# Windowed attention: the mask added in PSUM by VectorE, and the reciprocal denominators turned once and spread by DMAs

## The chip, the core and the metric

The kernel runs on one core of one Trainium2 chip. Its time is the device time of one execution in microseconds. A core has TensorE (matmuls and transposes, writing to PSUM), VectorE, ScalarE and GpSimd for elementwise work, and SyncE, which here only issues DMAs. The engines run their instructions in order and meet through semaphores.

## What is computed

Two layers of a diffusion trunk with 1,024 tokens of 1,024 features and 256 context tokens. Layer 0 mixes tokens by windowed attention with 16 query heads on 4 key/value heads, layer 1 by a Fourier mixer; each is followed by a mixture of 64 experts. The change is in layer 0's attention alone:

```
s = einsum('bqhgd,bkhd->bhgqk', qb, kk) * HEAD_DIM ** -0.5
s = where(abs(query - key) <= 128, s, -inf)          # window keys; context keys are unmasked
p = softmax(concatenate([s_window, s_context, sink], axis=-1))   # one sink logit per head, no value
out = p[window] @ v + p[context] @ v_ctx
y = out.reshape(B, L, 1024) @ w_o
```

## The kernel before

`attend` goes through 8 tiles of 128 queries and in each through 8 pairs of heads: 64 pairs. A pair has 384 window keys (256 in the first and last tile) and 256 context keys for each of its two heads. Pairs are even or odd, and each of the two kinds has its own PSUM buffer (`pair0`, `pair1`). A pair goes through these steps:

- TensorE: `scores(p)`, the products with the keys (L909 to L919) and then two bf16 matmuls with an identity, which add the mask of the outer key tiles (L923).
- VectorE: `largest(p, 0)` and `largest(p, 1)` (L795), the row maxima of the two heads, and `shift` (L804).
- ScalarE: `exps(p)`, two exponentials (L862) that write `prob` and its row sums.
- TensorE: `turn(p)`, ten transposes of 128x128 (eight in the edge tiles) into the same PSUM buffer (L934).
- VectorE and ScalarE: `copy(p)`, the first 512 columns and the rest to `pT` (L812, L870).
- TensorE: `values` (L954), once for two pairs: the part behind even pairs has twelve instructions in the trace, the part behind odd ones eight (four in the edge tiles).

The order is written out by hand. TensorE does `turn(p)`, at every fourth pair `denominators`, then `values`, then `scores(p + 2)`, which needs both copies of pair p. VectorE does `largest(p+1, 0)`, `copy(p)`, `largest(p+1, 1)`, `shift(p+1)`, and then at p = 2 of 4 `sinks`, at p = 3 of 4 `denominators`, at p = 1 of 4 `divide`. ScalarE does `copy(p)`, then `exps(p+1)`.

Four pairs are a group (8 heads), and there are 16. Its outputs lie transposed in PSUM (`att_o`, features on partitions, queries along the row), so its 8 reciprocal denominators per query must be brought into that shape. VectorE makes them (L827, 128x8), GpSimd spreads them to 128x512 (L782), TensorE transposes that in four pieces (`denominators`, L962), ScalarE copies it to `share` (`shares`, L879), and VectorE's `divide` multiplies (L833):

```
dve.wait_ge(share_done, n + 1)
dve.wait_ge(pv_mm, 4 * n + 4)
dve.tensor_tensor(oT[:, 4 * c:4 * c + 4, t * P:(t + 1) * P], psO[:], share[:], ALU.mult).then_inc(o_done, 1)
```

SyncE first loads `w_o` (L759), then fills scratch memory of the expert stages with zeros (L762 to L768), then loads the queries of tiles 2 to 7 (L754), each as soon as its buffer is free. When all engines have ended the attention, the next block begins with the output product (`mixY`, L1325).

Of the kernel before, what the change touches and what calls it, by code (L numbers as in the profile page):

```python
# [22 lines left out]
P = 128  # L23
D = 1024
# [179 lines left out]
def trunk(nc, A, out):  # L204
# [9 lines left out]
    with ExitStack() as whole:  # L214
# [481 lines left out]
        def attend(kT, v, w_o, oT, first_q, mask, sink):  # L696
# [6 lines left out]
            with ExitStack() as ctx:  # L703
                sb, ps, sem = pools(ctx)
                qT = first_q[:].rearrange("p (i k c) -> p i k c", i=2, k=KT)
                identb = sb("identb", [P, P], BF16)
# [4 lines left out]
                spread = sb("den_spread", [P, 4, 2, HD])  # L711
# [8 lines left out]
                far_mm, score_mm, max_done, exp_done = sem("far_mm"), sem("score_mm"), sem("max_done"), sem("exp_done")  # L720
                T_first, T_rest, copied_a, copied_d, pv_mm, o_done = (sem(n) for n in (
                    "probT_first", "probT_rest", "probT_a", "probT_d", "pv_mm", "o_done"))
                sink_in, sink_done, den_own, den_done, spread_done, den_mm, share_done = (sem(n) for n in (
                    "sink_in", "sink_done", "den_own", "den_done", "den_spread_done", "den_mm", "share_done"))
# [25 lines left out]
                with nc.Block(no_gpsimd_drain=True) as block:  # L750
                    @block.sync
                    def _(sp):
# [9 lines left out]
                        sp.dma_start(u_dram[DUMMY:, :].rearrange("p (h c) -> p h c", h=2),  # L762
                                     zero.unsqueeze(1).to_broadcast([P, 2, D // 2])).then_inc(zero_out, 16)
                        for l in range(DEPTH):
                            half = y_dram[l].rearrange("(n p j) (h c) -> j h p n c", p=P, j=2, h=2)
                            for h in range(2):
                                sp.dma_start(half[1, h], zero.unsqueeze(1).to_broadcast([P, YROWS // P, D // 2])).then_inc(zero_out, 16)
                                sp.dma_start(half[0, h, :, NT], zero).then_inc(zero_out, 16)  # L768
# [7 lines left out]
                    def _(pool):  # L776
                        pool.memset(zero, 0.0).then_inc(zeroed, 1)
                        pool.wait_ge(zeroed, 1)
                        for n in range(2 * NT):
                            pool.wait_ge(den_done, n + 1)  # L780
                            at_least(pool, den_mm, n)
                            pool.tensor_copy(spread[:], den[:].rearrange("p (a i) -> p i a", a=2).unsqueeze(3).to_broadcast([P, 4, 2, HD])  # L782
                                             ).then_inc(spread_done, 1)

                    @block.vector
                    def _(dve):
                        dve.tensor_copy(identb[:], ident[:]).then_inc(set_up, 1)
                        dve.tensor_scalar(nsink[:], sink[:], -1.0, None, ALU.mult).then_inc(set_up, 1)
                        dve.wait_ge(set_up, 2)

                        def largest(p, j):

                            dve.wait_ge(score_mm, p + 1)
# [26 lines left out]
                        def denominators(n):  # L820
# [3 lines left out]
                            at_least(dve, spread_done, n)  # L824
# [4 lines left out]
                        def divide(n):  # L829
                            t, c = n // 2, n % 2  # L830
                            dve.wait_ge(share_done, n + 1)
                            dve.wait_ge(pv_mm, 4 * n + 4)
                            dve.tensor_tensor(oT[:, 4 * c:4 * c + 4, t * P:(t + 1) * P], psO[:], share[:], ALU.mult).then_inc(o_done, 1)  # L833

                        largest(0, 0)
# [18 lines left out]
                    def _(act):  # L854
# [27 lines left out]
                        for p in range(N):  # L882
# [3 lines left out]
                            if p >= 4 and p % 4 == 0:  # L886
                                shares(p // 4 - 1)
# [1642 lines left out]
```

## Time and profile before

| | |
|---|---|
| Time, median of 3 runs | 2724.66 us (2721.68 to 2724.75) |
| Profiled execution | 2726.17 us, its span 2723.6 us |
| Granted TensorE clock, mean over the span | 0.985 |
| TensorE busy | 2614.6 us (96%) |
| VectorE, ScalarE, GpSimd busy | 2012.8, 1359.3, 613.1 us |
| The attention in the span | 253 to 520 us |

Starts are counted from the start of the span. Busy time of an engine is the time in which at least one of its instructions runs; matmuls overlap their neighbours, so the step from one start to the next is what one costs, and it is shorter than its duration. PE is TensorE, DVE VectorE, ACT ScalarE, POOL GpSimd, SPq the issuing of DMAs by SyncE. A clock of 1.00 is 2.4 GHz, 0.50 is 1.2 GHz.

### The profile page before, as it was taken

How to read it: one execution, taken by the hardware profiler on the slowest of the kernel's cores; microseconds unless marked ns; L12 is line 12 of the kernel's file. 1: busy time of each engine (PE TensorE's matmuls, PEld its weight loads, DVE VectorE, ACT ScalarE, POOL GpSimd, SP SyncE). 2: the span in 40 equal slices, each digit the busy share in tenths (PEclk: the TensorE clock that was granted, in tenths of full speed). 3: DMA queues.
4: the chain of work that ended last, by engine and by line, in shares of the span. 5: the costliest groups of instructions: out<-in, count | busy, mean ns of one | idle time of the engine just before them, and what ended most of it. 6: DMA issues, size and time to landing. Idle time of an engine off the chain costs nothing. (4 is left out here: it accounts for less than half of the span.)

```text
span 2723.6 us, 44405 instructions
## 1 busy us (share of the span) xinstructions
PE 2614.6 (96%) x14920; PEld 1176.8 (43%) x14923; DVE 2012.8 (74%) x5303; ACT 1359.3 (50%) x3150; POOL 613.1 (23%) x467
## 2 busy tenths in 40 slices
PE   7999999999899999999999889998999999999996
PEld 2444666544433333333444365444333343333342
DVE  4996666585588887788888465855898888888875
ACT  1112666343256666666666251431666666666651
POOL 0000000111023233233322221100233323233322
PEclk9999999999999999999999999999999999999998
DMA  9776500200399999999999732016999999999996
GB/s 366 266 266 200 187 17 17 76 39 39 146 371 368 332 337 353 327 337 377 352 334 339 248 146 84 39 47 241 362 366 340 343 318 341 335 372 332 338 345 205
DMA packets 151614, 697.65 MB, mean 256 GB/s; under 512 B 25505, under 2 KB 30881, under 8 KB 99162
## 3 DMA queue, kind: packets, MB, share of 16 engines
q1 hardware_dynamic: 103964, 555.09, 52.3%
q0 software_dynamic: 46832, 136.58, 20.3%
q10 hardware_dynamic: 592, 3.16, 0.3%
q8 instruction: 119, 1.95, 0.3%
q14 instruction: 107, 0.87, 0.1%
HBM read 597.50 MB, written 129.13 MB: 267 GB/s over the span
## 5 line engine op out<-in xcount | busy, mean ns | idle before, releaser
L1842 ACT ACTIVATE xT<-xt_blocks 32x256 f32<-32x256 f32 x2176 | 900.4, 414 | 39.0 <-DVE xt_blocks L1663 11.6
L1920 PE MATMUL exG<-ring,xT 128*32 128x512 f32 (+2 forms) x2608 | 572.1, 593 | 1.3 <-DMA ring<-in_exp_w_up_dram 0.7
L1678 DVE STREAM_TRANSPOSE ex_hT<-ex_h 32x64 f32<-32x64 f32 x2240 | 528.7, 236 | 33.6
L1920 PE MATMUL exG<-wide_w,xT 128*32 128x512 f32 (+2 forms) x1472 | 385.2, 600 | 0.7 <-DVE xT L1657 0.7
L1589 POOL DMA_INDIRECT y_scratch<-wide_w,idx_out x203 | 335.8, 1654 | 149.0 <-issue 66.6
L1920 PE MATMUL exG<-wide_t,xT 128*32 128x512 f32 (+2 forms) x960 | 361.5, 603 | 7.8 <-issue 4.4
L1576 POOL DMA_INDIRECT wide_t<-u_scratch,idx x144 | 152.6, 1060 | 937.8 <-DVE idx_out L1714 742.5
L1920 PEld LDWEIGHTS exG<-ring,xT 128*32 128x32 f32 (+2 forms) x2608 | 199.5, 129 | 314.7 <-issue 312.2
L1854 ACT ACTIVATE ex_e<-exG 128x256 f32<-128x256 f32 x142 | 54.4, 383 | 503.7 <-PE exG L1920 500.2
L1955 PE MATMUL exD<-ring,ex_hT 128*32 128x512 f32 (+2 forms) x1304 | 296.2, 597 | 2.5 <-DVE wide_w L1706 2.5
L1668 DVE TENSOR_TENSOR ex_h<-ex_e,exG 128x256 f32<-128x256 f32 x142 | 86.7, 611 | 190.9 <-ACT ex_e L1854 162.3
L1955 PE MATMUL exD<-wide_w,ex_hT 128*32 128x512 f32 (+2 forms) x736 | 197.4, 597 | 0.0
L1920 PEld LDWEIGHTS exG<-wide_w,xT 128*32 128x32 f32 (+2 forms) x1472 | 132.9, 134 | 146.9 <-issue 146.9
L1706 DVE SCALAR_TENSOR_TENSOR wide_w<-exD,w_all,mod 128x1024 f32<-128x1024 f32 x142 | 181.9, 1281 | 8.5 <-PE exD L1955 7.8
L1955 PE MATMUL exD<-wide_t,ex_hT 128*32 128x512 f32 (+2 forms) x480 | 181.9, 597 | 0.0
L1920 PEld LDWEIGHTS exG<-wide_t,xT 128*32 128x32 f32 (+2 forms) x960 | 111.0, 135 | 161.5 <-issue 158.8
L1628 DVE TENSOR_TENSOR mod<-place,slots 128x1024 bf16<-128x1024 f32 (+3 forms) x203 | 175.2, 888 | 3.5 <-PEq L235 2.5
L795 DVE TENSOR_REDUCE mx<-pair 128x1 f32<-128x640 f32 (+1 forms) x128 | 100.5, 786 | 95.0 <-PE pair L923 95.0
L1663 DVE STREAM_TRANSPOSE xt_blocks<-wide_t 128x1024 f32<-128x1024 f32 x136 | 168.1, 1236 | 2.3 <-DMA wide_t<-u_scratch,idx 2.3
L315 POOL TENSOR_TENSOR rstd<-var,halves 128x1 f32<-128x1 f32 x42 | 62.9, 1498 | 433.3 <-DVE var L301 433.3
L1955 PEld LDWEIGHTS exD<-ring,ex_hT 128*32 128x32 f32 (+2 forms) x1304 | 97.1, 129 | 115.7 <-issue 114.4
L1245 ACT ACTIVATE u2T<-mod 32x256 f32<-32x256 f32 x224 | 92.7, 414 | 108.1 <-DVE mod L1119 105.5
(369 smaller groups left out, 3275.8 us busy)
## 6 DMA issues: line engine op xcount, KB each, us to landing
ring<-in_exp_w_gate_dram SPq DMA_DIRECT2D x64, 1024.0 KB
ring<-in_exp_w_up_dram SPq DMA_DIRECT2D x64, 1024.0 KB
ring<-in_exp_w_down_dram SPq DMA_DIRECT2D x64, 1024.0 KB
wide_t<-in_exp_w_gate_dram SPq DMA_DIRECT2D x34, 1024.0 KB
wide_t<-in_exp_w_up_dram SPq DMA_DIRECT2D x34, 1024.0 KB
wide_t<-in_exp_w_down_dram SPq DMA_DIRECT2D x34, 1024.0 KB
wide_w<-in_exp_w_gate_dram SPq DMA_DIRECT2D x32, 1024.0 KB
wide_w<-in_exp_w_up_dram SPq DMA_DIRECT2D x32, 1024.0 KB
```

What stands on the lines that cost most here:

```text
L795: dve.tensor_reduce(mx[:, p % 2, j:j + 1], halves_of(p, pair[p % 2])[j], AX, ALU.max).then_inc(own, 1)
L1245: last = act.activation(uT[m * UNIT:(m + 1) * UNIT, t % DEEP, :, a * UNIT:(a + 1) * UNIT], parts[a * UNIT:(a + 1) * UNIT, m], ACT.Copy)
L1576: pool.indirect_dma_start(out=xg[:, par], out_offset=None, in_=u_dram, in_offset=bass.IndirectOffsetOnAxis(ap=idx[:, par:par + 1], axis=0) ...
L1589: pool.indirect_dma_start(out=y_dram[layer], out_offset=bass.IndirectOffsetOnAxis(ap=idx_out[0:at + n, par, j:j + 1], axis=0), in_=yo[0:at ...
L1628: last = dve.tensor_tensor(hot[:, par, :, at:at + n], place[:, :, r:r + 1].to_broadcast([P, NT, n]), slots[:, start:start + n].unsqueeze(1 ...
L1663: dve.transpose(xt[:], xg[:, par]).then_inc(blocks_done, 1)
L1668: dve.tensor_tensor(hid[:, par].rearrange("t (k p) -> t p k", k=FK), e[:].rearrange("t (p k) -> t p k", k=FK), psG[par][:, 1].rearrange("t ...
L1678: last = dve.transpose(hT[m * UNIT:(m + 1) * UNIT, par].rearrange("p (k t) -> p k t", k=FK)[:, :, a * UNIT:(a + 1) * UNIT], hid[a * UNIT:( ...
L1706: dve.scalar_tensor_tensor(out=yo[:, par], in0=psD[:].rearrange("p a b -> p (a b)"), scalar=w_all[:, ds(b, 1)], in1=gate2, op0=ALU.mult, o ...
L1842: last = act.activation(xT[m * UNIT:(m + 1) * UNIT, par, :, a * UNIT:(a + 1) * UNIT], parts[a * UNIT:(a + 1) * UNIT, m], ACT.Copy)
L1920: last = pe.matmul(psG[par][p:p + m], xT[:, par, k, p:p + m], ring[s % RING][:, 0:2, k * FF:(k + 1) * FF], start=k == 0, stop=k == KT - 1)
L1955: last = pe.matmul(psD[p:p + m, c], hT[:, b % 2, k * P + p:k * P + p + m], ring[s % RING][:, 2, k * D + c * 512:k * D + (c + 1) * 512], st ...
```

## The change

Two things change inside `attend`.

The two mask matmuls go. After the last score matmul VectorE adds the mask itself, in place in PSUM, for both heads in one 128x2x2x128 instruction (`cover`; 128x2x1x128 in the edge tiles), and the row maxima wait for it.

The reciprocals (128x8) are no longer spread by GpSimd. TensorE transposes them in one piece to 8x128, ScalarE copies these to 8 partitions of SBUF (`lift`, `den_rows`), and SyncE issues eight DMAs for a group (`share_of`), each of which copies one row of 128 numbers to 64 partitions of `share`. `divide` waits for all eight. The zero-filling DMAs and the query loads now stand between these in SyncE's order. TensorE no longer waits at its start for `identb`, which goes.

```diff
--- before.py
+++ after.py
                         sp.wait_ge(zeroed, 1)
-                        sp.dma_start(u_dram[DUMMY:, :]...).then_inc(zero_out, 16)
-                        for l in range(DEPTH):
...
-                        for t in range(2, NT):
-                            sp.wait_ge(score_mm, PAIRS * (t - 1))
-                            load(t)
+                        def share_of(n):
+                            sp.wait_ge(den_lifted, n + 1)
+                            at_least(sp, o_done, n)
+                            for h in range(8):
+                                a, i = divmod(h, 4)
+                                sp.dma_start(share[a * HD:(a + 1) * HD, i],
+                                             den_rows[h:h + 1].unsqueeze(1).to_broadcast([1, HD, P])).then_inc(share_in, 16)
+                        for n in range(2 * NT):
+                            if n % 2 == 1 and n + 3 < 2 * NT:
+                                t = (n + 3) // 2
+                                sp.wait_ge(score_mm, PAIRS * (t - 1))
+                                load(t)
+                            share_of(n)
+                            if n < 1 + 4 * DEPTH:
+                                clear(n)
 
                     @block.gpsimd
-                        for n in range(2 * NT):
-                            pool.wait_ge(den_done, n + 1)
-                            at_least(pool, den_mm, n)
-                            pool.tensor_copy(spread[:], den[:]...to_broadcast([P, 4, 2, HD])).then_inc(spread_done, 1)
 
                     @block.vector
-                        dve.tensor_copy(identb[:], ident[:]).then_inc(set_up, 1)
+                        def cover(p):
+                            t = p // PAIRS
+                            tiles, (W, S) = near_tiles(t), width(p)
+                            edge = [i for i, k in enumerate(tiles) if k != t]
+                            dve.wait_ge(score_mm, p + 1)
+                            both = pair[p % 2][:, 0:2 * S].rearrange("p (j s c) -> p j s c", j=2, c=P)[:, :, edge[0]:edge[-1] + 1:2]
+                            gone = mask[:, tiles[edge[0]] - t + 1:tiles[edge[-1]] - t + 2:2]
+                            dve.tensor_tensor(both, both, gone.unsqueeze(1).to_broadcast([P, 2, len(edge), P]), ALU.add).then_inc(masked, 1)
                         def largest(p, j):
-                            dve.wait_ge(score_mm, p + 1)
+                            dve.wait_ge(masked, p + 1)
                         def denominators(n):
-                            at_least(dve, spread_done, n)
+                            at_least(dve, den_mm, n)
                         def divide(n):
-                            dve.wait_ge(share_done, n + 1)
+                            dve.wait_ge(share_in, 128 * n + 128)
                         for p in range(N + 2):
                             if p + 1 < N:
+                                cover(p + 1)
                                 largest(p + 1, 0)
 
                     @block.scalar
-                        def shares(n):
+                        def lift(n):
                             act.wait_ge(den_mm, n + 1)
-                            at_least(act, o_done, n)
-                            act.activation(share[:], psR[:], ACT.Copy).then_inc(share_done, 1)
+                            at_least(act, share_in, 128 * n)
+                            act.activation(den_rows[:], psR[0:8, 0], ACT.Copy).then_inc(den_lifted, 1)
 
                     @block.tensor
-                        pe.wait_ge(set_up, 1)
                         def scores(p):
-                            for j in range(2):
-                                over = sc[j][:, 0:W].rearrange("p (s c) -> p s c", c=P)[:, edge[0]:edge[-1] + 1:2]
-                                last = pe.matmul(over, identb[:], mask[...], start=False, stop=True)
                             last.then_inc(score_mm, 1)
                         def denominators(n):
-                            pe.wait_ge(spread_done, n + 1)
-                            for i in range(4):
-                                last = pe.transpose(psR[:, i], spread[:, i].rearrange("p a d -> p (a d)"), ident[:])
-                            last.then_inc(den_mm, 1)
+                            pe.wait_ge(den_done, n + 1)
+                            at_least(pe, den_lifted, n)
+                            pe.transpose(psR[0:8, 0], den[:], ident[:]).then_inc(den_mm, 1)
```

How this moves instructions, first on VectorE in an inner tile, from the reciprocals of one group (`den`) to the division of the same group (`wide_t`, where the attention's output is kept); before:

```order
L825 TENSOR_TENSOR sink_exp_5<-row_sum_5,sink_exp_5 128x8
L827 RECIPROCAL den_5<-sink_exp_5 128x8
L795 TENSOR_REDUCE mx_5<-pair1_5 128x1
L812 COPY pT_5<-pair0_5 128x512
L795 TENSOR_REDUCE mx_5<-pair1_5 128x1
L804 SCALAR_TENSOR_TENSOR nm_5<-mx_5,nsink_5 128x2
L795 TENSOR_REDUCE mx_5<-pair0_5 128x1
L812 COPY pT_5<-pair1_5 128x512
L795 TENSOR_REDUCE mx_5<-pair0_5 128x1
L804 SCALAR_TENSOR_TENSOR nm_5<-mx_5,nsink_5 128x2
L833 TENSOR_TENSOR wide_t<-att_o_5,share_5 128x4x128
```

and in the changed kernel (L808 is `cover`, L814 `largest`, L831 `copy`, L823 `shift`, L852 `divide`):

```order
L846 RECIPROCAL den_5<-sink_exp_5 128x8
L808 TENSOR_TENSOR pair1_5<-pair1_5,mask_2 128x2x2x128
L814 TENSOR_REDUCE mx_5<-pair1_5 128x1
L831 COPY pT_5<-pair0_5 128x512
L814 TENSOR_REDUCE mx_5<-pair1_5 128x1
L823 SCALAR_TENSOR_TENSOR nm_5<-mx_5,nsink_5 128x2
L808 TENSOR_TENSOR pair0_5<-pair0_5,mask_2 128x2x2x128
L814 TENSOR_REDUCE mx_5<-pair0_5 128x1
L831 COPY pT_5<-pair1_5 128x512
L814 TENSOR_REDUCE mx_5<-pair0_5 128x1
L823 SCALAR_TENSOR_TENSOR nm_5<-mx_5,nsink_5 128x2
L852 TENSOR_TENSOR wide_t<-att_o_5,share_5 128x4x128
```

Each pair has one more instruction ahead of its first reduction; the division keeps its place. SyncE's queue, at the zero-filling of layer 0's scratch (`y_scratch0`), before:

```order
L767 DMA y_scratch0<-logits 128x9x512
L768 DMA y_scratch0<-logits 128x512
L767 DMA y_scratch1<-logits 128x9x512
L768 DMA y_scratch1<-logits 128x512
L767 DMA y_scratch1<-logits 128x9x512
L768 DMA y_scratch1<-logits 128x512
L754 DMA first_q_2<-qT_scratch 128x1024 x6
```

and in the changed kernel (L778 is `share_of`, L769 and L771 `clear`):

```order
L769 DMA y_scratch0<-logits 128x9x512
L778 DMA share_5<-den_rows_5 64x1x128 x8
L769 DMA y_scratch0<-logits 128x9x512
L754 DMA first_q_2<-qT_scratch 128x1024
L778 DMA share_5<-den_rows_5 64x1x128 x8
L771 DMA y_scratch1<-logits 128x512
L778 DMA share_5<-den_rows_5 64x1x128 x8
L771 DMA y_scratch1<-logits 128x512
```

What was issued in a row at the start of the attention is spread over its first nine groups, one zero-filling DMA behind each group's eight.

## Rows read from the trace of the kernel before

**Rows 1.** Windows in the attention: us, busy per engine, granted clock, DMA share, GB/s.

```profile
300.00:480.00 180.00, 180.00 (x1420) 119.54 (x1418) 110.77 (x215) 111.04 (x236) 6.75 (x11) 1.00 0.07 25
500.00:520.00 20.00, 17.39 (x132) 10.53 (x130) 11.12 (x24) 9.97 (x26) 1.23 (x2) 1.00 0.00 1
```

**Rows 2.** Timeline of one even pair, 358 to 367 us: start, us, engine, line.

```profile
358.40 0.37 PE L914 MATMUL pair<-kT,first_q 64*128 64x128 f32 x1
359.79 0.39 PE L923 MATMUL pair<-mask,identb 128*128 128x256 bf16 x2
360.02 1.25 PE L934 MATMUL pair<-ident,prob 128*128 128x128 f32 x10
360.22 0.82 DVE L795 TENSOR_REDUCE mx<-pair 128x1 f32<-128x640 f32 x1 [2.44 <-PE pair L923]
360.96 0.68 DVE L812 COPY pT<-pair 128x512 f32<-128x512 f32 x1
362.60 0.79 ACT L862 ACTIVATE prob<-pair,nm 128x640 f32<-128x640 f32 x1 [0.48 <-DVE nm L804]
363.84 1.35 PE L934 MATMUL pair<-ident,prob 128*128 128x128 f32 x10
366.56 0.37 PE L914 MATMUL pair<-kT,first_q 64*128 64x128 f32 x1
```

**Rows 3.** Timeline: one group's denominators and division; the even pair after.

```profile
356.42 0.60 PE L962 MATMUL att_den<-ident,den_spread 128*128 128x128 f32 x4
357.33 0.59 ACT L879 ACTIVATE share<-att_den 128x512 f32<-128x512 f32 x1
362.49 0.69 DVE L833 TENSOR_TENSOR wide_t<-att_o,share 128x512 f32<-128x512 f32 x1
375.17 0.37 PE L914 MATMUL pair<-kT,first_q 64*128 64x128 f32 x1
```

**Rows 4.** Groups by line and shape on VectorE: busy us, mean ns of one.

```profile
L833 DVE TENSOR_TENSOR wide_t<-att_o,share 128x512 f32<-128x512 f32 x16 | 11.1, 691 | 3.4 <-PE att_o L954 3.4
L1124 DVE TENSOR_TENSOR sh_e<-mixG,sh_e 128x256 f32<-128x256 f32 x16 | 6.5, 408 | 30.4 <-ACT sh_e L1269 30.1
L1225 DVE TENSOR_TENSOR wide_w<-mixY,moving 128x512 f32<-128x512 f32 x2 | 1.7, 842 | 1.3 <-ACT moving L1315 1.3
```

**Rows 5.** Issues of SyncE in the timeline; then the DMA view, us to landing.

```profile
0.72 0.40 SPq L425 DMA_DIRECT2D cond<-in_c_dram  x1
1.18 0.42 SPq L426 DMA_DIRECT2D cond<-in_c_ctx_dram  x1
253.12 2.82 SPq L759 DMA_DIRECT2D wide_w<-in_attn_w_o_dram  x4
cond<-in_c_ctx_dram SPq DMA_DIRECT2D x1, 4.0 KB, 1.9
u_scratch<-u SPq DMA_DIRECT2D x16, 512.0 KB, 2.6
```

**Rows 6.** Timeline: the attention's start, its first division, and its end.

```profile
253.16 0.56 DVE L787 CAST identb<-ident 128x128 bf16<-128x128 f32 x1 [3.16 <-PEq L235]
274.39 0.59 ACT L879 ACTIVATE share<-att_den 128x512 f32<-128x512 f32 x1
279.06 0.69 DVE L833 TENSOR_TENSOR wide_t<-att_o,share 128x512 f32<-128x512 f32 x1
515.39 0.20 DVE L827 RECIPROCAL den<-sink_exp 128x8 f32<-128x8 f32 x1
518.97 0.69 DVE L833 TENSOR_TENSOR wide_t<-att_o,share 128x512 f32<-128x512 f32 x1 [3.38 <-PE att_o L954]
520.60 9.68 PE L1325 MATMUL mixY<-wide_w,wide_t 128*128 128x512 f32 x22 [1.74 <-PEq L235]
```

**Rows 7.** Timeline and window: TensorE at the same place of layer 1.

```profile
1657.57 14.98 PE L1325 MATMUL mixY<-wide_w,wide_t 128*128 128x512 f32 x28 [4.63 <-PEq L235]
1660.00:1662.00 2.00, 2.00 (x4) 0.70 (x3) 0.00 (x0) 0.00 (x0) 2.00 (x2) 0.50 0.96 303
```

More of the change, by code:

```diff
@@ L710, in attend @@
                 share = sb("share", [P, 4, P])
-                spread = sb("den_spread", [P, 4, 2, HD])
+                den_rows = sb("den_rows", [8, P])
                 prob = sb("prob", [P, 2, 2, S])
@@ L720, in attend @@
                 far_mm, score_mm, max_done, exp_done = sem("far_mm"), sem("score_mm"), sem("max_done"), sem("exp_done")
+                masked = sem("masked")
                 T_first, T_rest, copied_a, copied_d, pv_mm, o_done = (sem(n) for n in (
                     "probT_first", "probT_rest", "probT_a", "probT_d", "pv_mm", "o_done"))
-                sink_in, sink_done, den_own, den_done, spread_done, den_mm, share_done = (sem(n) for n in (
-                    "sink_in", "sink_done", "den_own", "den_done", "den_spread_done", "den_mm", "share_done"))
+                sink_in, sink_done, den_own, den_done, den_mm, den_lifted, share_in = (sem(n) for n in (
+                    "sink_in", "sink_done", "den_own", "den_done", "den_mm", "den_lifted", "share_in"))
                 def heads(p):
@@ L760, in _ @@
                                              A["attn_w_o"][0, first:first + 4 * HD].rearrange("(i p) n -> p i n", p=HD)).then_inc(w_in, 16)
-                        sp.wait_ge(zeroed, 1)
-                        sp.dma_start(u_dram[DUMMY:, :].rearrange("p (h c) -> p h c", h=2),
-                                     zero.unsqueeze(1).to_broadcast([P, 2, D // 2])).then_inc(zero_out, 16)
-                        for l in range(DEPTH):
[L765 to L768, printed above, removed]
@@ L769, in _, with clear @@
-                        for t in range(2, NT):
-                            sp.wait_ge(score_mm, PAIRS * (t - 1))
-                            load(t)
+                        def clear(n):
+                            if n == 0:
+                                sp.dma_start(u_dram[DUMMY:, :].rearrange("p (h c) -> p h c", h=2),
+                                             zero.unsqueeze(1).to_broadcast([P, 2, D // 2])).then_inc(zero_out, 16)
+                                return
+                            l, j, h = (n - 1) // 4, (n - 1) // 2 % 2, (n - 1) % 2
+                            half = y_dram[l].rearrange("(n p j) (h c) -> j h p n c", p=P, j=2, h=2)
+                            if j == 1:
+                                sp.dma_start(half[1, h], zero.unsqueeze(1).to_broadcast([P, YROWS // P, D // 2])).then_inc(zero_out, 16)
+                            else:
+                                sp.dma_start(half[0, h, :, NT], zero).then_inc(zero_out, 16)
@@ L886, in _ @@
                             if p >= 4 and p % 4 == 0:
-                                shares(p // 4 - 1)
+                                lift(p // 4 - 1)
                             if p + 1 < N:
                                 exps(p + 1)
-                        shares(N // 4 - 1)
+                        lift(N // 4 - 1)
                     @block.tensor
                     def _(pe):
-                        pe.wait_ge(set_up, 1)
                         def scores(p):
@@ L911, in scores @@
                                 for j in range(2):
-                                    pe.matmul(sc[j][:, 0:W], q[j], near[j], start=True, stop=False)
+                                    last = pe.matmul(sc[j][:, 0:W], q[j], near[j], start=True, stop=True)
                             else:
@@ L918, in scores @@
                                 for j in (1, 0):
-                                    pe.matmul(sc[j][:, 0:W], q[j], near[j], start=True, stop=False)
-                            edge = [i for i, k in enumerate(tiles) if k != t]
-                            for j in range(2):
-                                over = sc[j][:, 0:W].rearrange("p (s c) -> p s c", c=P)[:, edge[0]:edge[-1] + 1:2]
-                                last = pe.matmul(over, identb[:], mask[:, tiles[edge[0]] - t + 1:tiles[edge[-1]] - t + 2:2], start=False, stop=True)
+                                    last = pe.matmul(sc[j][:, 0:W], q[j], near[j], start=True, stop=True)
                             last.then_inc(score_mm, 1)
```

8 lines of the change are left out of this document (2 added, 6 removed).

## Prediction

> **What bounds it now.** I read the windows first. Between 300 and 480 us, the six inner token tiles, TensorE is busy in all of the 180 us and VectorE and ScalarE in 111 each, at clock 1.00 [rows 1]. That looks like a kernel in which any work taken off TensorE is won. The timeline shows otherwise. Follow one even pair: its scores start on TensorE at 358.40, the first reduction at 360.22 (1.82 later), the copy at 360.96 (0.74), the first exponential at 362.60 (1.64: the copy, the second reduction and the shift), its ten turning transposes at 363.84 (1.24) and the scores of the next even pair, in the same PSUM buffer, at 366.56 (2.72: transposes and twelve value matmuls). The round takes 8.16 [rows 2]. It is a closed chain through three engines: its ten transposes take 1.35 where the unhurried ten at 360.02 take 1.25 [rows 2], so TensorE already waits a tenth there for the second exponential. The next even round, with the denominators in it, runs from 366.56 [rows 2] to 375.17 [rows 3]: 8.61. Both together are 16.77 per group of four pairs. So TensorE's own work and this chain are equally long, and a saving on the one that lengthens the other is a loss.
>
> **Term 1, the mask, 48 inner pairs.** Off TensorE: two bf16 matmuls, 359.79 to 360.02, 0.23 a pair. The scores are then whole when the last score matmul is: I put VectorE's start at 359.90, 1.50 after 358.40 instead of 1.82, an estimate from these two rows (0.32 earlier: 0.23 and part of the mask's own 0.39) [rows 2]. Then comes the new addition, 128x512 with one operand in PSUM. I find no VectorE write to PSUM in the trace. Nearest are the division (PSUM times SBUF, 512 wide, 0.69) and a strided 512-wide one at 0.84; 256 wide takes 0.41 [rows 4]. I take 0.69 and 0.03 for the wait on itself, since the division has the same width and a PSUM operand; bounds 0.60 (0.69 without part of its fixed cost) and 0.84. The chain grows by 0.69 + 0.03 - 0.32 = 0.40 a round, with the bounds 0.31 and 0.55.
>
> The Trainium skill ("VectorE: DVE Perf Modes", the TRN2 errata section) gives PSUM-source operations 120 + FD cycles at 0.96 GHz, 0.66 us for 512 elements; the row says 0.69, and the measurement decides. By the page term 1 would be some 0.7 us smaller.
>
> **Term 2, the denominators.** Four transposes of 0.60 together [rows 3] become one, some 0.15 to 0.20: 0.40 less in one of the two even rounds. GpSimd's spreading copy goes too, which nobody in the middle waits for. Terms 1 and 2: 2 x 0.40 - 0.40 = +0.40 per group, times 12 groups = **+4.8** (bounds +2.6 and +8.4). The 16 edge pairs have a 256-wide addition of 0.41 [rows 4] and lose a mask of half the width; about +0.2 a round against -0.40 a group, so nothing.
>
> **Term 3, the DMAs.** ScalarE's 128x512 copy becomes an 8x128 one, 0.3 by the 0.59 of the wide one [rows 3], then SyncE issues eight DMAs, and the division, on VectorE, waits for all. SyncE's small issues stand 0.46 apart (0.72, 1.18), its larger ones of four pieces 0.70 (2.82 for four); the second small one landed 1.9 after its issue, a 512 KB one after 2.6 [rows 5]. I take 0.50, near the small ones, and 1.9. In the middle: 357.33 + 0.30 + 0.05 + 7 x 0.50 + 1.9 = 363.1, where the division starts at 362.49 now [rows 3]. VectorE is next needed for the odd pair's addition, at about 363.7 (its scores start near 362.2; 1.50 on), and the division takes 0.69: done at 363.8, a tenth late, and on an odd pair. An odd round has eight value matmuls instead of twelve; the 2.72 behind 363.84 [rows 2] less 1.28 for the transposes is 1.44 for twelve, so four are 0.5 us of slack. Middle groups: **0**. In the edge tiles less time lies between: 274.39 to 279.06, 4.67 instead of 5.16 [rows 3, 6]. There 274.39 + 5.75 = 280.1 is 1.0 late, for three groups (the first and two in the last tile): **+3**. Behind the waiting division stand the next pair's addition and its reductions on VectorE, for which the exponentials and TensorE wait. On SyncE the zero-filling DMAs and the query loads now stand between the share DMAs; both fit into the 16.8 us between two groups, and nobody in the attention waits for the zeros.
>
> The Trainium skill ("DMA: Bandwidth & Descriptors", Anatomy of one DMA and Rules for kernel authors) speaks against this step: a fixed 2.0 us per DMA before bytes / 436 GB/s, and small transfers should be coalesced. Its 2.08 for 32 KB against the 1.9 of my row would add under 1 us to the total, at the edges and the end.
>
> **Term 4, the end.** Nothing covers the last group. The reciprocal ends at 515.59; now the last division starts at 518.97 and layer 0's output product at 520.60 [rows 6]. Then: transpose and copy to 516.2, eight DMAs to 516.25 + 3.5 + 1.9 = 521.7. **+2.7.**
>
> **Term 5, the clock.** TensorE's value matmuls then end near 517.9 and the product starts near 523.3: a pause over 5 us, where it is 1.74 now. The same product in layer 1 starts after a pause of 4.63, and its window shows clock 0.50, that is 1.2 GHz: 28 matmuls in 14.98, 0.535 each [rows 7], against 0.44 each (22 in 9.68) after the short pause [rows 6]. 28 x 0.095 = **+2.7**, and VectorE waits for that product, so it is carried on. Inside the attention the clock holds: it is 1.00 in a window with TensorE busy 17.4 of 20 [rows 1], and I expect above 85%.
>
> **Term 6, the start.** TensorE no longer waits for the 0.56 cast [rows 6]: **-0.5**.
>
> Sum: 4.8 + 0 + 3 + 2.7 + 2.7 - 0.5 = **+12.7**. The profiled span 2723.6 becomes 2736.3; that execution took 2726.17 in all, 1.5 above the median of the runs, to which I add the same 12.7: 2724.66 + 12.7 = 2737.4, said as 2737.
>
> **Rivals.** (a) *The DMAs come late everywhere*, chance 0.20. For: the four-piece issues have 0.70; eight at 0.66 (most of that) and a landing of 2.6 [rows 5] give 357.66 + 4.6 + 2.6 = 364.9, division done at 365.6, 1.9 late. The odd pair's slack takes 0.5, so 1.4 x 12 = 17, 4 more at the edges and 2 at the end: +36, 2761. Every step between is possible: at 0.60 apart it is 0.7 later, 0.3 x 12 + 2 + 0.7 = 6 more than the forecast, +19, 2744. Against: a share DMA has one dimension less than those. (b) *Faster, since TensorE binds*, chance 0.07. If the even rounds have slack that I don't see, up to 48 x 0.23 + 16 x 0.12 + 16 x 0.40 = 19 us go from TensorE, and terms 3 to 6 give back 7.9: -11, 2714. It decides at half a us of such slack, or at an addition of 0.16 (12 x (2 x -0.13 - 0.40) = -7.9). Against: the transposes' 1.35 beside 1.25, and no 512-wide row below 0.69. (c) *Within 0.2%*, chance 0.13: the addition at 0.60 (+2.6), DMAs 0.42 apart, which is the issue's own duration (edges within the slack, +2.1 at the end), and a pause that leaves the clock alone: 2.6 + 2.1 - 0.5 = +4, 2729. (d) The forecast, +5.5 to +20, chance 0.60.
>
> **Numbers.** 0.2% is 5.4 us, about what can be told from no change. Slower: (a) and (d), 0.80; within, 0.13; faster 0.07. The range 2728 to 2757 leaves out (b), the upper end of (a) and a little of (c).
>
> **What would show it.** The added operation's mean near 0.69; reductions of the middle starting 2.2 after their pair's scores; groups of 17.2 us where they are 16.8; TensorE below 100% in the middle, waiting for the exponentials; VectorE's division waiting for a DMA by tenths in the middle, about 1 us at the edges and 6 at the end; clock 0.50 at the first output product. The prediction is wrong if an issue of the share DMAs takes above 0.6 or their landing above 2.3, if the addition is far from 0.69, or if the odd rounds have less slack than I think.

## The result and the profile after

The changed kernel takes 2844.45 us (median of 4 runs, 2841.89 to 2847.97) where the kernel before takes 2724.7 on the same chip: a ratio of 1.0438, with a 95% interval of 1.0423 to 1.0454. It is slower by some 120 us; 2737, and at most 2757, was predicted. The profiled span is 2846.1 us, the granted clock 0.965 on the mean.

The page's rows of TensorE show where to look first. Six of the 40 slices have a clock below 9 tenths; the last one has it in the kernel before too, and the other five lie over the attention.

```profile
PE   7998777769989999999999978999899999999996
PEclk9999888879999999999999999999999999999998
```

The same window as in [rows 1] (us, busy us of PE, PEld, DVE, ACT and POOL with counts, granted clock, DMA share, GB/s):

```profile
300.00:480.00 180.00, 135.99 (x910) 84.00 (x910) 97.17 (x178) 76.88 (x167) 0.00 (x0) 0.86 0.41 70
```

TensorE was busy in all of these 180 us, and now it is in 136, at a clock of 0.86; every engine does less in them. The chain of one group of four pairs, in the timeline from one group's `den_rows` to the next group's issues, answers to [rows 3]:

```profile
396.65 0.25 ACT L900 ACTIVATE den_rows<-att_den 8x128 f32<-8x128 f32 x1
396.92 6.09 SPq L778 DMA_DIRECT2D share<-den_rows  x8
407.89 0.69 DVE L852 TENSOR_TENSOR wide_t<-att_o,share 128x512 f32<-128x512 f32 x1 [5.92 <-DMA share<-den_rows]
408.73 2.83 PE L969 MATMUL att_o<-pT,v 128*64 128x256 f32 x12 [4.13 <-DVE wide_t L852]
411.49 0.58 PE L933 MATMUL pair<-kT,first_q 64*128 64x128 f32 x1
419.38 0.27 PE L976 MATMUL att_den<-ident,den 128*8 128x128 f32 x1
419.58 1.52 PE L969 MATMUL att_o<-pT,v 128*64 128x256 f32 x12
420.57 6.01 SPq L778 DMA_DIRECT2D share<-den_rows  x8
```

Read it in order. The eight DMAs are issued over 6 us, 0.76 for each (6.09 / 8). The division can start only 10.97 us after the first issue (396.92 to 407.89), and VectorE had stood still for 5.92. Then comes what the prediction never priced. The next group's first value matmuls write into the one accumulator `att_o` that the division reads, so TensorE waits for the division, 4.13 here. After that pause twelve value matmuls take 2.83 where they take 1.52 at 419.58, and a score matmul 0.58 for 0.34 to 0.37: TensorE runs at half the clock for a while, as the windows behind the pause and after it show (the granted clock is the third number from the end):

```profile
408.70:411.50 2.80, 2.77 (x14) 1.39 (x14) 2.73 (x5) 0.00 (x0) 0.00 (x0) 0.50 0.00 0
413.70:419.00 5.30, 4.75 (x37) 3.12 (x36) 4.68 (x9) 2.47 (x5) 0.00 (x0) 1.00 0.00 0
```

From one group's issue to the next one's are 23.65 us, 23.86 in the group before (373.06 to 396.92); it was 16.77.

Over the whole kernel, first the share DMAs by their line, then VectorE's division by its line (idle before it, who waited for it):

```profile
L778 SPq DMA_DIRECT2D share<-den_rows x128: 463/598/1352, 278.5 to 628.3; - x128
DMA to landing us min/median/max: 2.7/4.7/6.0
```

```profile
  DMA share<-den_rows: 103.7, 16
  PE att_o L969: 66.2, 15
```

The median of 4.7 hides a queue. In nearly every group the first DMA lands 3.3 us after its issue, the second after 4.1, the last after 5.7 (median of the groups); the landings of a group follow each other at some 1.1 us, and the last is 11.1 behind the first issue. At the last group nothing else is moved, and the DMA view of 621 to 634 us, 40 equal slices, shows at what pace: 24 to 28 GB/s in nearly all slices, with one burst shortly before the fourth and the fifth DMA land, 0.25 us apart.

```profile
GB/s 0 0 0 0 0 0 0 0 0 28 28 24 25 24 27 24 25 25 25 25 25 25 25 38 133 32 24 24 25 25 24 24 21 24 24 27 10 0 0 0
```

At 25 GB/s the 32 KB of one DMA take 1.3 us (an estimate from this row), while the next is issued 0.5 to 0.64 us later. So they pile up. The issuing itself is held up too: the first six of the group at 396.92 start 0.51 to 0.64 apart, the last two 1.1 and 1.3.

The added instruction costs what was expected; groups by line and shape, busy us and mean ns of one:

```profile
L808 DVE TENSOR_TENSOR pair<-pair,mask 128x512 f32<-128x512 f32 x48 | 33.5, 697 | 48.6 <-PE pair L938 48.6
L808 DVE TENSOR_TENSOR pair<-pair,mask 128x256 f32<-128x256 f32 x16 | 6.9, 430 | 15.6 <-PE pair L931 15.6
```

The end, beside [rows 6]:

```profile
622.82 6.05 SPq L778 DMA_DIRECT2D share<-den_rows  x8
633.29 0.69 DVE L852 TENSOR_TENSOR wide_t<-att_o,share 128x512 f32<-128x512 f32 x1 [11.97 <-DMA share<-den_rows]
634.93 15.86 PE L1338 MATMUL mixY<-wide_w,wide_t 128*128 128x512 f32 x32 [9.27 <-PEq L235]
```

From here on "the attention" is the time from TensorE's first score matmul to the start of this product. Before it lasts from 253.78 to 520.60, 266.8 us; now from 255.15 to 634.93, 379.8: **+113.0** of the 120. The product itself takes 15.86 where its 32 matmuls took 13.97 (+1.9), and the attention began 1.4 later. The 3 us or so that remain lie in other stages and were not traced.

### The profile page after: what moved, and what is told of

Same layout as the page of the kernel before. It is cut to its first block and busy times, and to the rows that moved or that the text cites. A ratio compares the mean times of both kernels' runs of the same rounds, so it can differ in the third digit from the quotient of the medians.

```text
span 2846.1 us, 44228 instructions
## 1 busy us (share of the span) xinstructions
PE 2642.1 (93%) x14744; PEld 1181.4 (42%) x14747; DVE 2052.7 (72%) x5366; ACT 1355.7 (48%) x3150; POOL 604.5 (21%) x451
## 5 line engine op out<-in xcount | busy, mean ns | idle before, releaser
L1719 DVE SCALAR_TENSOR_TENSOR wide_w<-exD,w_all,mod 128x1024 f32<-128x1024 f32 x142 | 181.9, 1281 | 10.1 <-PE exD L1968 9.5
L969 PE MATMUL att_o<-pT,v 128*64 128x256 f32 x608 | 100.9, 471 | 66.2 <-DVE wide_t L852 66.2
L1968 PEld LDWEIGHTS exD<-ring,ex_hT 128*32 128x32 f32 (+2 forms) x1304 | 96.9, 129 | 116.9 <-issue 115.8
```

What stands on the lines that cost most here:

```text
L969: last = pe.matmul(psO[a * HD:(a + 1) * HD, 2 * half:2 * half + 2], v[:, slot(t, j), kv * HD:(kv + 1) * HD], heads_T[:, :, j * P:(j + 1) * ...
L1719: dve.scalar_tensor_tensor(out=yo[:, par], in0=psD[:].rearrange("p a b -> p (a b)"), scalar=w_all[:, ds(b, 1)], in1=gate2, op0=ALU.mult, o ...
L1968: last = pe.matmul(psD[p:p + m, c], hT[:, b % 2, k * P + p:k * P + p + m], ring[s % RING][:, 2, k * D + c * 512:k * D + (c + 1) * 512], st ...
```

## The experiments

The chips differ by some us, so each time stands beside that of the kernel before on its own chip. Three of the kernels don't divide by the right denominators; where they are told, that is said. The attention is always measured in the one profiled execution; in the kernel before it takes 266.8 us. Lines left out of an edit are marked by dots.

**One part at a time.** In the first kernel the mask is added by VectorE, and the denominators go as before; in the second the denominators go by transpose and DMAs, and the mask stays on TensorE.

```diff
 e1_mask_only, against the kernel before
-                                last = pe.matmul(over, identb[:], mask[...], start=False, stop=True)
...
+                                cover(p + 1)
 e2_den_only, against the changed kernel
-                                cover(p + 1)
...
+                                last = pe.matmul(over, identb[:], mask[...], start=False, stop=True)
```

> The mask is added by VectorE as in the changed kernel; the denominators go the old way (GpSimd's spreading copy, four transposes, ScalarE's copy). Theory (the division's wait for the DMAs makes nearly all of the loss): each even round grows by 0.40 and no transposes are saved, 24 x 0.40 = 9.6, about 1 more in the edge tiles, 0.5 less at the start: some +10 us, 2735. Rival (the in-place addition in PSUM is what costs, through the wait that it adds ahead of every reduction): at least +50 us.

> The denominators go the new way (one transpose, eight DMAs per group); the mask is still added by TensorE's matmuls. Theory: the division waits some 6 us in each of 16 groups as in the changed kernel, so about +105 to +115 us, 2835. Rival (the mask is the cause): within 10 us of the kernel before. Rival (the two together make the loss, since only the longer chain exposes the wait): about +50.

The mask alone: 2738.01 beside 2723.12, ratio 1.0045 (1.0027 to 1.0063); the attention takes 278.5, +11.7. GpSimd's copy marks the groups, 17.61 us apart, 0.84 more than 16.77:

```profile
359.74 0.61 POOL L782 COPY den_spread<-den 128x512 f32<-128x512 f32 x1 [17.00 <-DVE den L835]
377.35 0.61 POOL L782 COPY den_spread<-den 128x512 f32<-128x512 f32 x1 [17.00 <-DVE den L835]
```

The denominators alone: 2836.32, ratio 1.0411 (1.0391 to 1.0431), attention 374.8, +108.0, with the same pattern in the chain of waits:

```profile
DVE wide_t L844 <- DMA share<-den_rows: 109.9, 16, 11.4
PE att_o L965 <- DVE wide_t L844: 73.0, 15, 5.8
```

So nine tenths of the loss lie in the DMAs' path. The two alone add up to 119.7, 6.7 more than both together. This fits a VectorE that waits for a DMA anyway, so that a part of its additions is free: its wait falls from 109.9 without them to 103.7 with them.

**What makes the DMAs late, and who pays.** e3 lets each of the eight DMAs read 64 partitions of a block of ones instead of one partition 64 times. e4 leaves the DMAs as they are, but lets them write to an unused buffer, while the division takes ones that stand ready.

```diff
 e3_spread_source
-                                             den_rows[h:h + 1].unsqueeze(1).to_broadcast([1, HD, P])).then_inc(share_in, 16)
+                                             ones[0:HD, :]).then_inc(share_in, 16)
 e4_no_wait
-                                sp.dma_start(share[a * HD:(a + 1) * HD, i],
+                                sp.dma_start(aside[a * HD:(a + 1) * HD, i],
...
-                            dve.wait_ge(share_in, 128 * n + 128)
```

> The changed kernel, but each share DMA reads 64 rows of 128 ones from 64 partitions of SBUF instead of one row of one partition 64 times; same destination, same number of descriptors, same bytes, same waits (the division by the denominators is left out in effect, since the shares are all one). Theory (reading everything from one partition limits the DMA: 64 packets of 512 B in 1.05 us are 31 GB/s): eight issues at 0.60 and a landing near 2 us, 6.5 us from lift to division instead of 10.4, so some 3.5 to 4 us less in each of 16 groups, about 2785. Rival (a fixed cost per DMA or per packet, whatever the source): 2844 as the changed kernel.

> The changed kernel with all its DMAs, but they write a buffer that nobody reads, and the division reads shares that were set to one ahead of the loop and doesn't wait for the DMAs (the division by the denominators is left out in effect). The stage still ends only when the last eight have landed. Theory: the wait alone is the loss. What stays is terms 1 and 2 (+4.8), the end (eight DMAs in 10.4 us, +7.7) and the cold product (+2): +14, 2739. Rival (the DMAs' traffic, or the clock, slows other work): at least +30.

Neither divides by the denominators. The whole kernels then take 3555 and 3546 us, since other values go into the stages behind, so only the attention can be compared. e3: 292.4, +25.6, which is 87 us less than in the changed kernel, where 3.5 to 4 in each of 16 groups were expected; e4: 284.0, +17.2. In the DMA view (KB each, median us to landing), e3 and then e4:

```profile
share<-ones SPq DMA_DIRECT2D x128, 32.0 KB, 1.9
```

```profile
aside<-den_rows SPq DMA_DIRECT2D x128, 32.0 KB, 4.5
```

The same bytes in the same 512-byte pieces land after 1.9 from 64 partitions and after 4.5 from one. The first DMA of a group, with no other in front of it, shows what the source alone does: some 2 us (1.8 to 2.3) in e3 and 3.3 in e4. In e3 no queue builds up, and the last landing is 6.3 behind the first issue instead of 11. And in the middle the slow DMAs cost nothing by themselves: in e4 all of them run, and with nobody waiting the groups are 17.28 apart.

**The source, with the full computation.** Here each reciprocal stands 16 times in the transpose's input, so that a head's row comes to lie on 16 partitions and each DMA reads these 4 times. The run beside it keeps the source on one partition and moves a quarter of the columns (the rest of `share` holds 1.0; only its attention, of a single execution, is comparable).

```diff
 e5_sixteen_rows
+                            dve.reciprocal(den16[:], es[:].unsqueeze(2).to_broadcast([P, 8, 16])).then_inc(den_done, 1)
...
+                                             den_rows[16 * h:16 * h + 16].unsqueeze(1).to_broadcast([16, 4, P])).then_inc(share_in, 16)
 e6_quarter_rows
+                                sp.dma_start(share[a * HD:(a + 1) * HD, i, 0:32],
+                                             den_rows[h:h + 1, 0:32].unsqueeze(1).to_broadcast([1, HD, 32])).then_inc(share_in, 16)
```

> The changed kernel, but the reciprocals are repeated 16 times before the transpose, so that the row of each head stands on 16 partitions and each of the eight DMAs reads 16 partitions 4 times instead of one partition 64 times. Same bytes, same number of DMAs and of 512-byte packets, full computation. If reading one partition over and over is what makes the DMAs slow: landing 1.9 to 2.6 us as with the source of 64 partitions (e3), the division's wait down from 104 to about 35 us, attention +25 (at most +35) over before, total about 2755. Rival, it is the number of small packets: landing stays at 4.5 or more, attention stays at +100 or more, total about 2840.

> The changed kernel, but each of the eight DMAs moves only 32 of the 128 columns (64 packets of 128 bytes from one partition); the other columns keep 1.0, so the output is not divided rightly and the later stages are not comparable; only the attention is read. If the bytes read from one partition set the time: landing about 2.5 (2 fixed and a quarter of 2.7), attention +35 or less. If each packet from the same partition has a fixed price: landing stays between 4 and 5 and attention near +110.

e5: 2759.87 beside 2729.31, ratio 1.0105 (1.0088 to 1.0122); attention 297.4, +30.6. The landing is 2.0 in the median, and in the group at 331.52 for all eight alike; eight issues take 5.0 instead of 6.0, and TensorE's clock is 1.00 again:

```profile
share<-den_rows SPq DMA_DIRECT2D x128, 32.0 KB, 2.0
```

```profile
300.00:480.00 180.00, 163.03 (x1202) 101.62 (x1202) 138.05 (x239) 100.69 (x219) 0.00 (x0) 1.00 0.28 88
```

e6: landing 2.0 too, attention 294.7, +27.9:

```profile
share<-den_rows SPq DMA_DIRECT2D x128, 8.0 KB, 2.0
```

Both ways out work: 64 pieces from one partition are fine if they are short (128 bytes), and 512-byte pieces are fine if they come from 16 partitions. So neither the number of pieces nor the single partition alone makes the DMAs slow, but many bytes out of one partition do. The 4.7 is not the price of one such DMA: alone it takes 3.3, 1.3 or so more than the 2.0 of a fast one, and the rest is the wait behind those in front. With 8 KB each nothing piles up, and the landing is below the 2.5 that was expected.

Of e5's +30.6 a part stays. The last landing is 6.4 to 7.5 behind the first issue, and VectorE still waits 37.3 in 16 groups; the groups are 17.79 apart (331.52 to 349.31 in its issues), and later ones mostly 18.1 to 18.9, for a reason that was not traced. And the sixteen copies aren't free: the reciprocal now writes 128 columns instead of 8 and takes 0.95 instead of 0.20.

```profile
L847 DVE RECIPROCAL den<-sink_exp 128x128 f32<-128x128 f32 x16 | 15.2, 953 | 0.5
```

**Two queues.** GpSimd issues the four DMAs that write partitions 64 to 127 of `share`, SyncE the four that write 0 to 63.

```diff
-                            for h in range(8):
+                            for h in range(4):
...
+                            for i in range(4):
+                                pool.dma_start(share[HD:2 * HD, i],
+                                               den_rows[4 + i:5 + i].unsqueeze(1).to_broadcast([1, HD, P])).then_inc(share_pool, 16)
```

> The changed kernel, but four of the eight DMAs are issued by GpSimd at the same time as the other four by SyncE. If the pace of issue on one queue (0.76 us each, 6.0 for eight) and the landing add up, the last landing comes 3 us earlier: division's wait 3 us shorter in 15 groups, attention about +70, total about 2800. Rival, the DMAs' service is the limit whoever issues them: the landing gets later as the issue gets earlier (6 to 8 us), attention stays within 10 us of +113, total 2835 to 2845; GpSimd's issue may be slower than SyncE's.

2772.27 beside 2729.31, ratio 1.0160 (1.0143 to 1.0177); attention 310.0, +43.2. My theory (+70) named the right direction and far too small a gain, and the rival (landings of 6 to 8, within 10 us of +113) fell. In the medians the landings are no later:

```profile
share<-den_rows SPq DMA_DIRECT2D x64, 32.0 KB, 4.5
share<-den_rows POOLq DMA_DIRECT2D x64, 32.0 KB, 4.6
```

The medians mislead, for each queue now holds four DMAs instead of eight. Place by place the four land after 3.3, 4.1, 4.7 and 4.7 in the one queue (the group at 396.92) and after 3.5, 3.9, 5.5 and 6.0 on SyncE, 3.4, 4.1, 5.1 and 5.6 on GpSimd (the group at 372.73). So the two queues do hold each other up a little, but they mostly run side by side: all eight have landed 7.8 us behind the first issue instead of 11.1. Whether it is one partition that gives its bytes slowly or a few neighbours together is open, since the eight sources lie on partitions 0 to 7 in both kernels.

The division's wait falls from 103.7 to 50.5, by 3.3 us in each of 16 groups, which accounts for 53 of the 70 us won. The clock is 1.00 between 300 and 480 us. The 17 that are left are near the 16 that the clock is found to be worth below; here they were not told apart.

**The wait taken off the path.** The DMAs stay as they are. The accumulator gets a second buffer and the division stands two rounds later, so that only the last group waits for a landing.

```diff
-                psO, psR = ps("att_o", [P, 4, P]), ps("att_den", [P, 4, P])
+                psO = ps("att_o", [P, 2, 4, P])
...
-                            if p >= 5 and p % 4 == 1:
+                            if p >= 7 and p % 4 == 3 or p == N + 1:
                                 divide(p // 4 - 1)
...
-                                    at_least(pe, o_done, 2 * t + c)
+                                    at_least(pe, o_done, 2 * t + c - 1)
```

> The changed kernel with the DMAs as they are, but the accumulator of the value products in two buffers and the division two rounds later, so that nothing waits 10 us for the landing except the last group; the one transpose writes into the buffer not in use. Full computation. Theory, the wait for the landing (with the slow clock it brings) is the whole loss in the middle: no wait of the division there, clock 1.00, attention +11.7 (as with the mask alone) and +5 to +8 at the end, total 2740 to 2748. Rival, the slow DMAs also hold the clock or the engines down by themselves: attention stays over +50, clock under 0.95.

2745.80 beside 2729.31, ratio 1.0058 (1.0042 to 1.0075); attention 283.1, +16.3. In the middle the clock is 1.00 and the groups are 17.29 apart, as in e4:

```profile
344.54 6.23 SPq L778 DMA_DIRECT2D share<-den_rows  x8
361.83 6.04 SPq L778 DMA_DIRECT2D share<-den_rows  x8
```

```profile
536.02 0.69 DVE L852 TENSOR_TENSOR wide_t<-att_o,share 128x512 f32<-128x512 f32 x1 [11.37 <-DMA share<-den_rows]
537.65 15.85 PE L1339 MATMUL mixY<-wide_w,wide_t 128*128 128x512 f32 x32 [10.71 <-PEq L235]
```

The first two lines are the issues, the last two the end. The rival (slow DMAs hold the engines or the clock down by themselves) is out. At the end the product waits 10.71 where it waited 1.74 [rows 6]: +9.0.

**The clock by itself.** The changed kernel, with 32 transposes of no use in TensorE's gap before the value matmuls, 3.7 us a group, from the second group on.

```diff
...
+                                        for _ in range(32):
+                                            pe.transpose(psR[:, 1], ident[:], ident[:])
                                     at_least(pe, o_done, 2 * t + c)
```

> The changed kernel with nothing else moved, but from the second group on TensorE does 32 transposes of the identity (some 4 us, results unused) in the gap in which its value products wait for the division. It adds work and takes no wait away. Theory, the pause costs twice: the wait itself, and a lower granted clock (0.86) for the work between the waits: with the gap filled the clock stays near 1.00 in the middle, a group takes about 22 us where it took 23.9, the attention is +80 to +95 over before instead of +113, total about 2815. Rival, the low clock is not of the pause but of the DMAs, or costs nothing: clock stays at 0.86 or the time stays at 2844 or grows by the filler.

2826.09 beside 2725.56, ratio 1.0367 (1.0348 to 1.0385): with more work it is faster than the changed kernel, whose ratio is 1.0438. The attention takes 363.7, +96.9, just outside the +80 to +95 expected. VectorE's wait is unchanged, the value matmuls take 1.52, and the clock is 1.00 (the last of the lines):

```profile
DVE wide_t L852 <- DMA share<-den_rows: 104.3, 16, 11.2
```

```profile
355.79 0.69 DVE L852 TENSOR_TENSOR wide_t<-att_o,share 128x512 f32<-128x512 f32 x1 [6.22 <-DMA share<-den_rows]
356.53 1.52 PE L973 MATMUL att_o<-pT,v 128*64 128x256 f32 x12 [0.85 <-DVE wide_t L852]
300.00:480.00 180.00, 156.80 (x1205) 107.05 (x1204) 102.82 (x189) 79.56 (x174) 0.00 (x0) 1.00 0.45 83
```

A group takes 22.54 (333.25 to 355.79, from division to division) instead of 23.88 (336.79 to 360.67). The 1.3 between them is as much as the twelve slow value matmuls lose, 2.83 - 1.52.

**A version without either wait, and its control.** The mask stays on TensorE; groups 0 to 14 go through the one transpose and the DMAs, with two accumulators and the later division; the last group goes through GpSimd's copy and the four transposes. The control is the kernel before with two accumulators and the later division only.

```diff
 e10_last_by_pe
...
+                            if n < N // 4 - 1:
+                                pe.transpose(psO[0:8, (n + 1) % 2, 0], den[:], ident[:]).then_inc(den_mm, 1)
+                            else:
+                                pe.wait_ge(spread_done, 1)
+                                for i in range(4):
+                                    last = pe.transpose(psO[:, (n + 1) % 2, i], spread[:, i].rearrange("p a d -> p (a d)"), ident[:])
```

> What is left when both waits are taken out: the mask stays on TensorE as before, the denominators of groups 0 to 14 go through the one transpose and the eight DMAs with the division two rounds later and two accumulators, and the last group goes through the four transposes as before. Full computation. If the four transposes of a group really are on the path: TensorE has 0.96 us less to do in each of 15 groups, of which I expect 0.4 to show: 5 us less than before, at most 14, total 2711 to 2722. Rival, TensorE waits for VectorE or ScalarE in those rounds anyway: same as before within 0.2%.

> Control for the run beside it: the kernel before with two accumulators and the division two rounds later and nothing else, all denominators through the four transposes. If the later division is neutral by itself: the time of before within 0.2% (2720 to 2729). If it gives something by itself, the gain of the other run is to be read against this one.

e10: 2719.62 (9 runs) beside 2725.56 (20 runs), ratio 0.9975 (0.9965 to 0.9986), attention 261.8, **-5.0**. e11: ratio 1.0000 (0.9989 to 1.0010), attention 266.8. So the later division alone gives nothing, and the gain is that of the shorter way of the denominators: three transposes fewer on TensorE, ScalarE's copy 8x128 instead of 128x512 and no copy on GpSimd, which were not told apart. In e10 the groups are 16.45 apart, in e11 16.78.

```profile
355.63 6.01 SPq L780 DMA_DIRECT2D share<-den_rows  x8
372.08 6.12 SPq L780 DMA_DIRECT2D share<-den_rows  x8
```

```profile
337.09 0.65 DVE L833 TENSOR_TENSOR wide_t<-att_o,share 128x512 f32<-128x512 f32 x1
353.87 0.65 DVE L833 TENSOR_TENSOR wide_t<-att_o,share 128x512 f32<-128x512 f32 x1
```

## Why the prediction was wrong

The failed step is term 3: it put the DMAs at 0.50 apart and 1.9 to the landing, with nothing to wait for in the middle groups, and the runs showed a last landing 11 us behind the first issue and a wait in all 16 groups. It failed by more than the whole sum, and term 5's last sentence fell with it. The direction came out as forecast, and terms 1 and 2 and, roughly, term 5 at the product hold. Term 6 can't be seen in the runs.

The +113.0 of the attention come apart in three steps, each the difference of two runs. Everything but the waits of the groups before the last is in e7: +16.3, of which 9.0 are the end. The waits at full clock are e9 less e7: 96.9 - 16.3 = 80.6, or 5.4 for each of 15 groups. The clock is the changed kernel less e9: 113.0 - 96.9 = 16.1. The last two are not wholly clean, since the filler takes TensorE's time too where a wait is short, and each attention is that of one execution.

- **Term 1, the mask: right.** The addition was put at 0.69, with 0.40 for each even round, 0.80 a group. It takes 0.697, and e1's groups are 0.84 longer. In the edge tiles the mask was put at 0.2 for each of 8 even rounds, 1.6 in all; 12 x 0.84 is 10.1 of e1's 11.7, which leaves 1.6 for them and the ends.
- **Term 2, the transposes: right.** -0.40 a group was predicted; 17.61 - 17.29 = 0.32 from e1 to e7, and 16.77 - 16.45 = 0.32 from the kernel before to e10, ScalarE's shorter copy included in both. Terms 1 and 2 together are +0.52 a group (17.29 - 16.77) instead of +0.40. This bears out the reading of the middle as a closed chain: taking the mask matmuls off TensorE lengthened the groups, although TensorE was busy in all of the 180 us.
- **Term 3, the DMAs: the failed step.** It said 0.50 apart and 1.9 to the landing, 5.4 in all, and nothing in the middle. They are 0.76 apart and land after 4.7 in the median; the division starts 11 us after the first issue. Both numbers are beyond the 0.6 and 2.3 that the prediction itself named as signs of being wrong. The sum `7 x 0.50 + 1.9` also takes for granted that a DMA lands as soon as the first one does, however many are in front of it. That holds in e5 (2.0 for all eight of the group at 331.52); here the first lands after 3.3 and the last after 5.7. The 1.9 came from a 4 KB load [rows 5], which reads nothing over and over. The prediction's own bounds, with the 2.6 of a 512 KB transfer at the upper end, did not reach this, for none of those rows had one partition as the source of 32 KB; e3 and e5 show that spreading the source takes it away, and e6 that fewer bytes do. What the bounds needed was a term for the shape of the source, and no row of before gave one.
- **Term 3 again: who waits behind the late division.** The text named VectorE's additions and reductions. It left out that the division frees the one accumulator, for which TensorE's next value matmuls wait: 66.2 us in 15 waits. e7, with a second accumulator and a later division, takes both kinds of wait away together; their shares were not told apart.
- **Rival (a)** had the mechanism, late DMAs in all groups, with 0.66 and 2.6, and +36. e5 is near that case (0.63 and 2.0) and lost 30.6. The mechanism was the right one with a chance of 0.20; its size was wrong by a factor of three, because the landing was and because TensorE's wait for the accumulator and the clock were left out.
- **Term 4, the end:** +2.7 predicted, +9.0 in e7, by the same landing and pace.
- **Term 5, the clock:** +2.7 at the product against 15.86 - 13.97 = +1.9. But "inside the attention the clock holds" rested on waits of tenths. With pauses of 4 to 5 us in every group it is 0.86 there, and this cost some 16 us. It is a consequence of term 3: in e5, e7 and e8 it is 1.00.
- **Term 6, the start:** TensorE no longer waits for the cast, but the attention began 1.4 later. Over all runs its start lies between 252.4 and 255.3, so half a us can't be seen there; what moves it was not looked for.

The Trainium skill ("DMA: Bandwidth & Descriptors", Anatomy of one DMA) gives 2.0 us and bytes / 436 GB/s for GpSimd's path, by which 32 KB take 2.08, an estimate. The DMAs of the runs, issued by SyncE, agree where the source is spread (1.9 in e3, 2.0 in e5) and not where it is one partition (3.3 for the first of a group, 4.7 in the median), and the measurement decides. That the Trainium skill's figure and my row agreed at 2 us was no evidence for this shape.

## What to carry to other kernels

Before a row is spread over partitions by DMA, look at its source: a landing time holds only for a source of the same shape and for a queue that keeps up. Here one partition that was read over and over made the first landing 1.3 us later and the median more than twice as long, because each DMA took longer than the step to the next issue. Several copies of the row on several partitions, which the same one transpose can give, took that away, for 0.75 us more in the reciprocal. So look at the landing of the first DMA of a burst and of the last one, and not at the median. Where a small transfer is put between two engines, follow its consumer one step further, to the buffer that the consumer frees, and count the pauses that it opens on TensorE twice, once as time and once as clock. And a saving that is worth 0.3 us a group, as here, showed only in the version in which the latency that it brings stood wholly beside other work, at the last group too.

## What the hardware showed beyond expectation

- Eight DMAs of 32 KB, each 64 reads of 512 bytes from one partition of SBUF, move at 24 to 28 GB/s. The first lands after 3.3 us, the last after 5.7, 11.1 behind the first issue. From 16 partitions (e5) each lands after 2.0, from 64 (e3) after 1.9, and with pieces of 128 bytes from one partition (e6) after 2.0.
- Two issuing queues (e8) run mostly side by side: all eight have landed after 7.8 us. At the same place in its queue a DMA lands up to 1.3 us later than with one queue (in the two groups compared above).
- The issues of such DMAs in one queue start 0.5 to 0.64 us apart up to the sixth; the seventh and the eighth come 1.1 and 1.3 later (the group at 396.92). With the fast landings of e5 the eight of the group at 331.52 are all 0.6 apart.
- After a pause of 4 to 5 us in a group twelve of TensorE's matmuls took 2.83 us instead of 1.52 (the granted clock was 0.50 there, and 0.86 instead of 1.00 over the window), and a kernel with 15 x 32 useless transposes in these pauses was faster by 16 us in the attention.
- VectorE's addition in place in PSUM takes 0.70 us for 512 columns (0.43 for 256), as much as its product of PSUM and SBUF into SBUF.
